# A hybrid attention and mixture-of-experts step on one Trainium2 core: expert 1's up weights issued earlier, the slot-weight product moved, the last down weights in quarters

## The reference, cut to what matters

```
combine = zeros((n, 16)).at[rows[:, None], eid].add(w)        # two experts of each token, with weights
for e in range(N_EXPERTS):                                    # 16 experts, hidden width 512
    h = jax.nn.silu(xt @ w_gate[e]) * (xt @ w_up[e])
    y = y + combine[:, e:e + 1] * (h @ w_down[e]).astype(jnp.float32)
...
y_prompt = _rms(xp, final_norm_g)                             # final norm, gain of 1024 values
```

## Time and profile before

| | |
|---|---|
| median of 3 runs | 741.18 us (738.06 to 742.09) |
| profiled execution | 742.04 us, span 740.4 us |
| TensorE busy | 688.3 us, 93% of the span |
| DVE, ACT, POOL busy | 261.9, 184.0, 140.2 us |
| chain that ended last | PE 77%, DMA 12% (10% of it the down weights), DVE 6% |
| moved by DMA | 185.66 MB, mean 251 GB/s |

### The profile page before, as it was taken

How to read it: one execution, slowest core, us unless ns; L and a number is a source line. 1 busy time by engine, 2 the same in 40 slices (tenths; PEclk the granted TensorE clock), 3 DMA queues, 4 the chain that set the end, 5 groups by cost and what they waited for, 6 DMA issues and landing times.

```text
span 740.4 us, 14741 instructions
## 1 busy us (share of the span) xinstructions
PE 688.3 (93%) x5443; PEld 445.6 (60%) x5443; DVE 261.9 (35%) x805; ACT 184.0 (25%) x459; POOL 140.2 (19%) x226
## 2 busy tenths in 40 slices
PE   4999999999997897998999979999999999999786
PEld 2475597749555465556555569965568775565332
DVE  4156311047245757663435462111121101121106
ACT  3110203012134944583413011001110010111104
POOL 0404016310341477000100110011111111111100
PEclk9999999999999998999999877999999999999989
DMA  9996148243677368103691159989999999999963
GB/s 344 371 307 218 39 137 269 90 138 115 211 241 293 96 177 232 69 2 115 269 395 55 46 187 355 359 323 393 363 397 408 387 362 379 360 375 400 370 259 125
DMA packets 56114, 185.66 MB, mean 251 GB/s; under 512 B 9103, under 2 KB 30896, under 8 KB 50019
## 3 DMA queue, kind: packets, MB, share of 16 engines
q1 hardware_dynamic: 44050, 152.54, 54.6%
q0 software_dynamic: 11984, 32.11, 14.3%
HBM read 172.97 MB, written 14.32 MB: 253 GB/s over the span
## 4 chain that ended last, share of the span: by engine, by line
PE 77%; DMA 12%; DVE 6%; ACT 3%; issue 1%; SPq 0%; DVEq 0%; ACTq 0%
PE ps L651 71%; DMA ring<-in_w_down_dram 10%; PE ps L899 2%; PE ps L1168 1%; DMA ring<-in_w_out_dram 1%; DMA ring<-in_w_in_dram 1%; PE ps L926 1%; PE ps L746 1%; ACT tabs L1545 1%; PE ps L802 0%; DVE ugr L1916 0%; DVE tabs L1940 0%; DVE vnr L2082 0%; DVE xr L2078 0%; PE ps L1044 0%
## 5 line engine op out<-in xcount | busy, mean ns | idle before, releaser
L651 PE MATMUL ps<-ring,xr 128*128 128x512 f32 (+3 forms) x640 | 138.4, 413 | 9.7 <-DMA ring<-in_w_in_dram 9.7
L651 PEld LDWEIGHTS ps<-ring,xr 128*128 128x128 f32 (+1 forms) x640 | 68.1, 151 | 72.0 <-issue 58.8
L651 PE MATMUL ps<-ring,work 128*32 128x128 f32 (+2 forms) x512 | 73.8, 376 | 2.2 <-DMA ring<-in_w_out_dram 1.6
L651 PE MATMUL ps<-ring,vnr 128*64 128x256 f32 (+1 forms) x1024 | 73.0, 328 | 0.0
L414 POOL DMA_DIRECT2D ring<-in_sel_pages_dram x96 | 51.4, 536 | 90.5 <-issue 57.0
L651 PE MATMUL ps<-ring,qT 128*32 128x256 f32 (+2 forms) x304 | 59.3, 516 | 4.9 <-DMA ring<-in_w_down_dram 4.9
L651 PEld LDWEIGHTS ps<-ring,vnr 128*64 128x64 f32 (+1 forms) x1024 | 49.6, 123 | 23.6 <-issue 6.8
L2411 DVE COPY vnr<-ps 128x256 f32<-128x256 f32 (+2 forms) x16 | 8.5, 533 | 153.5 <-PE ps L1168 153.5
L651 PE MATMUL ps<-ring 128*128 128x128 f32 (+1 forms) x512 | 59.6, 279 | 0.0
L651 PEld LDWEIGHTS ps<-ring 128*128 128x128 f32 x512 | 58.8, 191 | 0.3 <-issue 0.2
L2672 POOL DMA_INDIRECT x_rows<-kvn,qbd x14 | 20.7, 1479 | 199.6 <-DVE kvn L2457 67.2
(11 more groups left out here) (384 smaller groups left out, 807.0 us busy)
## 6 DMA issues: line engine op xcount, KB each, us to landing
ring<-in_w_gate_dram SPq DMA_DIRECT2D x11, 2048.0 KB
ring<-in_w_up_dram SPq DMA_DIRECT2D x11, 2048.0 KB
ring<-in_w_down_dram SPq DMA_DIRECT2D x11, 2048.0 KB, 26.9
xr<-in_w_gate_dram SPq DMA_DIRECT2D x5, 2048.0 KB, 24.7
tabs<-in_w_up_dram SPq DMA_DIRECT2D x5, 2048.0 KB, 27.6
ring<-in_cmp_pages_dram SPq DMA_DIRECT2D x64, 128.0 KB, 5.0
ring<-in_cmp_pages_dram POOLq DMA_DIRECT2D x64, 128.0 KB, 5.4
ring<-in_w_in_dram SPq DMA_DIRECT2D x3, 2048.0 KB, 9.2
```

What stands on the lines that cost most here:

```text
L651: return nc.tensor.matmul(out, lhsT, rhs, start=start, stop=stop)
```

## The change

Five edits, and several semaphores merged into others (`w1_in` into `pe_in`, `ss_ready` into `rs_ready`, `pcmp_h` into `hc_ready`, `peb_mm` into `comp_mm`, `gates_zero` into `gate_ready`, `hrep_ready` into `pcomp_ready`), which changes the counts waited for. The merges free four more semaphores for the quarters.

1. SP issues the up slab of expert 1 directly behind its gate slab, without the wait for `xe_in0`.
2. TensorE makes `weights_in_slots` between the second and third quarter of the first gate product, and no longer before the first row turn.
3. DVE makes the weight table in a function of its own, `placed_weights`, behind `overflow_flag`.
4. The last down slab comes in four loads with a semaphore each, and TensorE waits for each quarter before its products.
5. `gf` has two halves, at the ends of `ugr` and `vnr`, loaded when tile 4's mixed rows have been turned; the final norms of tiles 0, 1 and 4 work in halves.

```
-            load(ring[:, 0:2, :], t["w1"], "w1_in")
+            load(ring[:, 0:2, :], t["w1"], "pe_in")
...
+            sp.wait_ge(sem("mix_used"), ORDER.index(PT) + 1)
+            for n in range(2):
+                load(gf[n], t["gf"][:, W * n:W * n + W].to_broadcast([P, W]), "vectors_in")
             sp.wait_ge(sem("out_mm"), 2 * TILES)
             gate_in_turn(1, 1)
-            sp.wait_ge(sem("xe_in0"), 16)
             up_in_turn(1, 1)
             sp.wait_ge(sem("x2_out"), 16 * (TILES + 1))
             sp.wait_ge(sem("experts_placed"), 1)
...
                 after(sp, "y_mm", 2 * n - 4)
+                if n == E - 1:
+                    for f in range(FE):
+                        load(down_slots[n % 3][f], slab("w_down", placed[n])[:, D * f:D * f + D], "wd_last%d" % f)
+                    return
...
-            sp.wait_ge(sem("last_rows"), 2)
-            load(gf, t["gf"].to_broadcast([P, D]), "vectors_in")
             down_in_turn(E - 1)
...
             te.wait_ge(sem("weights_ready"), 1)
-            weights_in_slots()
...
                     for f in range(FE):
+                        if in_turn and n == 0 and bank == 2 and f == FE // 2:
+                            weights_in_slots()
                         for k in range(KD):
...
                 for f in range(FE):
+                    if n == E - 1:
+                        te.wait_ge(sem("wd_last%d" % f), 16)
...
+
+            def placed_weights():
+
                 dve.wait_ge(sem("slot_mm"), 2)
                 in_order(pb[7][:, 128:128 + E])
...
                     overflow_flag()
+                    placed_weights()
                     dve.wait_ge(sem("slots_ready"), 3)
...
-                    V.scalar_tensor_tensor(out=x2[0:rows, i, :], in0=x2[0:rows, i, :], scalar=rs,
-                                           in1=gf[0:rows, :], op0=ALU.mult, op1=ALU.mult).then_inc(sem("out_ready"), 1)
+                    for n in range(2):
+                        v = x2[0:rows, i, W * n:W * n + W]
+                        ins = V.scalar_tensor_tensor(out=v, in0=v, scalar=rs, in1=gf[n][0:rows, :],
+                                                     op0=ALU.mult, op1=ALU.mult)
+                    ins.then_inc(sem("out_ready"), 1)
```

More of the change, by code:

```diff
@@ L332, in hybrid_layer @@
         NORMED = [NORM_ORDER.index(i) for i in range(TILES)]
-        gf = work[:, 0:1024]
+        gf = [buf[:, PT * W:TILES * W] for buf in (ugr, vnr)]
         y_last = tabs[:, 1024:2048]
@@ L657, in position_bias @@
                 te.wait_ge(sem("cst_in"), 16)
-                te.wait_ge(sem("pe_in"), 64)
+                te.wait_ge(sem("pe_in"), 80)
                 for k in range(KD):
@@ L670, in compress @@
                 if s == 0:
-                    te.wait_ge(sem("w1_in"), 16)
+                    te.wait_ge(sem("pe_in"), 80)
                 else:
@@ L849, in compressed_scores @@
                 if c == 0:
-                    te.wait_ge(sem("pcomp_ready"), 2)
+                    te.wait_ge(sem("pcomp_ready"), 3)
                 else:
@@ L930, in _ @@
             project(1)
-            te.wait_ge(sem("ss_ready"), 1)
+            te.wait_ge(sem("rs_ready"), 1)
             for i in range(PT):
@@ L943, in _ @@
             turned(TILES - 1)
-            te.wait_ge(sem("rs_ready"), 1)
+            te.wait_ge(sem("rs_ready"), 2)
             compress(0)
@@ L965, in _ @@
             te.wait_ge(sem("turn_out"), 3 * TILES)
-            te.wait_ge(sem("hrep_ready"), 1)
+            te.wait_ge(sem("pcomp_ready"), 1)
             for g in range(G):
@@ L1204, in down @@
                 else:
-                    te.wait_ge(sem("wd_in%d" % par), 16 * (turn - E // 2 + len(range(par, E, 3)) + 1))
+                    te.wait_ge(sem("wd_in%d" % par), 16 * (turn - E // 2 + len(range(par, E - 1, 3)) + 1))
                     wv = down_slots[par]
@@ L1246, in light_down @@
                 te.wait_ge(sem("h_ready"), n + 1)
-                te.wait_ge(sem("wd_in%d" % (n % 3)), DOWN_LOADS[n % 3] * (n // 3 + 1))
+                if n < E - 1:
+                    te.wait_ge(sem("wd_in%d" % (n % 3)), DOWN_LOADS[n % 3] * (n // 3 + 1))
                 te.wait_ge(sem("y_out0"), n - 1)
@@ L1572, in _ @@
             compress(1)
-            act.wait_ge(sem("gates_zero"), 1)
+            act.wait_ge(sem("gate_ready"), 1)
             for n in range(2 * TILES, 3 * TILES):
@@ L1586, in _ @@
                   pb[6 + c][:, 128:144].rearrange("p (i g b) -> p i g b", g=G, i=PT), ACT.Gelu_apprx_tanh,
-                  bias=peb[:, c:c + 1]).then_inc(sem("pcmp_h"), 1)
+                  bias=peb[:, c:c + 1]).then_inc(sem("hc_ready"), 1)
             projected(4 * TILES)
-            act.wait_ge(sem("comp_mm"), 1)
+            act.wait_ge(sem("comp_mm"), 2)
             for n in range(2):
@@ L1800, in link @@
                 dve.wait_ge(sem("dve_step"), chain[0])
-            V.memset(gates[:, :, :], 0.0).then_inc(sem("gates_zero"), 1)
+            V.memset(gates[:, :, :], 0.0).then_inc(sem("gate_ready"), 1)
             link(V.memset(qbd[:, :, :], 0.0))
@@ L1813, in _ @@
                 link(V.tensor_tensor(sq[0], sq[0], sq[k], ALU.add))
-            dve.sem_inc(sem("ss_ready"), 1)
+            dve.sem_inc(sem("rs_ready"), 1)
             dve.wait_ge(sem("rs_mm"), 1)
@@ L1822, in position_bias @@
             def position_bias():
-                dve.wait_ge(sem("pe_in"), 64)
-                dve.wait_ge(sem("w1_in"), 16)
+                dve.wait_ge(sem("pe_in"), 80)
                 for l in range(32):
@@ L2083, in combine @@
                 dve.wait_ge(sem("combined"), pair + 1)
-            dve.wait_ge(sem("pcmp_h"), 2)
+            dve.wait_ge(sem("hc_ready"), 10)
             V.tensor_copy(hrep.rearrange("p (g h n) -> p g h n", g=G, h=HPG),
                           hp[:, 1, :].rearrange("p (g n) -> p g n", g=G)[:, :, None, :].to_broadcast([P, G, HPG, PBLK])
-                          ).then_inc(sem("hrep_ready"), 1)
-            dve.wait_ge(sem("comp_mm"), 1)
+                          ).then_inc(sem("pcomp_ready"), 1)
+            dve.wait_ge(sem("comp_mm"), 2)
             V.tensor_copy(kcs[:, :], pb[6][:, 0:256]).then_inc(sem("comp_ready"), 1)
-            dve.wait_ge(sem("comp_mm"), 2)
+            dve.wait_ge(sem("comp_mm"), 3)
             link(V.memset(kcp[:, :], 0.0))
@@ L2100, in _ @@
                             ).then_inc(sem("pcomp_ready"), 1)
-            dve.wait_ge(sem("pcomp_ready"), 2)
+            dve.wait_ge(sem("pcomp_ready"), 3)
             small_scores(0)
```

15 lines of the change are left out of this document (7 added, 8 removed).

## The result

| | before | after |
|---|---|---|
| median (lowest to highest), 4 runs each | 740.17 us (738.06 to 742.09) | 754.50 us (751.40 to 757.97) |
| profiled execution, span | 742.04, 740.4 us | 755.02, 753.3 us |

The ratio is 1.0182, 95% interval 1.0153 to 1.0211: slower, as forecast, but by 14.3 us where 5.5 were forecast, and 4.5 us above the end of the range. The span grew by 12.9 us.

The account below looks back on a forecast made before the run. TensorE was taken to set the pace until gate 5's load at 495.7 us, then a full DMA stream. Late row turn 6.2 + weights 2.3 - tail 3.0 = +5.5 us, giving 746.7 us; range 739.5 to 750.

Parts of the forecast that it names:

- The store lands 4.8 us late, the gather is issued 4.6 us late: Last h_rows store, beside up 1: lands at 443.9 us instead of 439.1; expert 0's gather issued at 444.85 us.
- The gather takes 2.5 us more: Expert 0's gather, beside gate 2 and up 2: 2.5 us more than its 4.4 us, landing at 451.7 us.
- Equal shares: Store and gather share evenly with weight loads: TensorE 2.3 us late, sum +1.6, 742.8 us; 30% together with no contention.
- 739.6: Time in us if store and gather meet no contention at all, sum -1.6; 30% together with equal shares.
- 732.9: Time in us if transfers bound everything: early load saves 5.3 us, with the tail -8.3; chance 15%.
- The rule on turns: Skill page: each DMA engine takes one packet in turn from each queue with work; equal shares would make contention far cheaper.
- The row turn gains 0.9 us without the small passes: Expert 0's row turn: taking the ten weight products from ahead of it gains only 0.9 us.
- The weights product costs 2.3 us: Middle of the first gate product: 20 small passes at full clock cost 2.3 us, bounds 2.3 to 4.7.
- The third rival: Clock falls twice: +1.8 us behind weights in mid product, +1.3 as the tail gains only 1.7; 749.8 us, chance 10%.
- TensorE's delay passes one to one into the end of the stream: TensorE's 8.5 us delay after gate product 0 lasts to gate 5's load and passes whole into the stream's end.
- The tail gains 3.0 us: Last down product waits for DVE, starts 1.7 us sooner, takes 3.65 us at full clock, ends at 719.15 us.
- The other edits cost nothing: Renamed semaphores cost nothing; row loads land in time; halved final norms, 0.13 us more apiece, run beside waits for ScalarE.

Follow-up runs that it names:

- e9: Changed kernel with the loads of up 1, gate 2 and up 2 in two pieces each, rows of 8 KB instead of 16: 745.78 us, ratio 1.0068.
- e7: Changed kernel with the loads of up 1, gate 2 and up 2 in four pieces each, rows of 4 KB instead of 16: 741.04 us, ratio 1.0018.
- e2: Kernel before with only the early load of expert 1's up slab, and the merged semaphores: 751.88 us, ratio 1.0155.
- e3: Kernel before with only the moved weights product and weight table, and the merged semaphores; up load held: 743.07 us, ratio 1.0041.
- e4: Kernel before with only the last down slab in quarters and early gf, and the merged semaphores; up load held: 738.00 us, ratio 0.9976.
- e11: Kernel before with only the last down slab in quarters, gf loaded late, and the merged semaphores: 737.67 us, ratio 0.9972.
- e1: Changed kernel with the wait for xe_in0 put back ahead of expert 1's up load, all else as changed: 739.99 us, ratio 0.9996.
- e12: Changed kernel with up 1, gate 2 and up 2 in four pieces and the weights product ahead of the row turn again: 739.17 us, ratio 0.9988.
- e10: Changed kernel with the up load held and the ten weight products ahead of the first gate product's last quarter: 741.27 us, ratio 1.0021.
- e5: Changed kernel with gate 2 and up 2 held until expert 0's rows are gathered, up 1 still early: 745.68 us, ratio 1.0078.

## Why the prediction was wrong in size

The place, the order of the steps and the sign were right; the sum of 5.5 us was mis-sized in two terms, and the larger one, the gather's, rested on a wrong rate.

- *The store lands 4.8 us late, the gather is issued 4.6 us late.* Measured 4.1 and 3.8 beyond the shift of 2.2 that the run had already. Right in size, with some luck: I let the first store (`x_rows`) land as before and the second 6.1 us after it. In fact the first took 11.4 us instead of 8.9, and the second landed 2.9 us after it (442.5 and 445.4 us).
- *The gather takes 2.5 us more.* Wrong: 7.3 more. This step failed. I took the 6.1 us between two landings in the earlier trace rows as the time of 512 KB under load. But both stores were under way in most of that stretch: the pair moved 1.05 MB in 17.2 us, 61 GB/s, not the 84 that 6.1 us make. At 61 GB/s the gather's 0.36 MB take 5.9 us; it took 11.7. For 7.1 us of these its packets moved, holding half as much as the stores', and a packet, not a byte, is what gets a turn; that its first packet would come 2.9 us later (4.6 us after the issue, 1.7 when alone) I had nowhere in the sum, and the cause of that stays open. The first error is one of reading, the second of a mechanism that I had not seen. The counts of packets and e9 show it, for the store e7 too; e2 shows the price of the early load.
- *Equal shares.* Its time, 742.8, was far off, as were 739.6 and 732.9. The rule on turns that I weighed and dropped holds in packets (183 to 180), not in bytes.
- *The row turn gains 0.9 us without the small passes.* As worked out, it starts where the gather lands.
- *The weights product costs 2.3 us.* Measured 4.0 in the profile: 2.5 for the passes and 1.6 for the clock, which I had kept for the range (1.8). The third rival had this half right; its other half, the clock in the tail, did not come. e3's median has +2.6, with an interval of 1.6 to 4.5 us.
- *TensorE's delay passes one to one into the end of the stream.* Gate 5 was 16.5 us late, the last up product 15.7 later (726.12, against 710.4 before: its 32 passes end a block of 64 that ends at 714.06): 0.8 us was made up on the way. Right.
- *The tail gains 3.0 us.* Measured 2.9, by the releaser and the duration that were named (DVE, 3.65 us). By the medians it is 2.5 in e4 and 3.2 in e11.
- *The other edits cost nothing.* e1 is level with before, though it holds the weights product (+2.6) and the tail (-2.5); within its interval (-1.9 to +1.4 us) nothing is left for the rest.

With 7.3 for 2.5 and 4.1 for 2.3 the sum is 3.8 + 7.3 - 0.9 + 4.1 - 2.9 = +11.4, 752.6 us by the same way of reckoning, inside the measured runs and 1.9 us under their median.

## What to carry to other kernels

A load that nobody waits for can still cost, through what it travels beside: before moving one into an empty stretch, look for small transfers on the critical path there, and for those that a delay pushes into the loads behind. Here weight loads with rows of 16 KB made a store take 10.0 us instead of 5.5 to 6.8 and a gather 11.7 instead of 4.4. Either hold them until it has landed, as the kernel before did, or cut their rows to its length, which gives back part of it (the store 7.4 us, expert 2's gather 8.3 instead of 10.5 to 12.6). Price such a meeting by packets, turn by turn, over the whole shared stretch, and not by the gap between two landings.

## What the runs showed of the hardware

- While both queues moved packets, they did so nearly one for one in the first gather and in the stores, whatever a packet held (180 to 183 in the changed kernel's gather beside 16 KB rows, 189 to 198 in e9's beside 8 KB rows, 216 to 215 in e7's stores beside 4 KB rows). Expert 2's gather had fewer turns, 112 to 142 in e1 and 112 to 194 in e7. From issue to landing this made 61 GB/s for the stores and 30 GB/s for the gather beside 16 KB rows, 90 GB/s for the gather alone (0.35 MB in 3.9 us, e1).
- The gather's first packet came 1.7 us after its issue when it was alone and 4.6 us after it beside 16 KB rows; in e7 it was 1.7 us for the first gather, with 4 KB rows still moving, and 4.2 for that of expert 2. What decides it is open.
- TensorE's granted clock fell to 0.50 in the middle of uninterrupted work, 2.6 to 3.0 us after 20 small passes of 128x16 had begun, where these began 0.5 to 0.8 us after its rise.
- The last down product took 3.65 us when 0.6 to 0.7 us of idle time stood ahead of it and 5.0 to 5.4 us with 1.9 to 2.6; but the last up product took 3.67 us after 2.2 us of idle in three profiles (after, e2, e12) and 5.36 after 2.2 and 2.5 in two (e10, e5).
- The fastest version was the tail alone, e11 at 737.67 us and e4 at 738.00 us, 0.2 to 0.3% under the kernel before.
